# Gates added into HBM cells by the transfers, the norm's factor moved ahead of the expert product, expert searches and row products started earlier

## The reference

```python
q = (xf @ w_q).reshape(n, PEER_HEADS, 2, PEER_DK // 2)
s = jnp.einsum('nhpd,hpkd->nhpk', q, sub_keys).astype(jnp.float32)
sv, si = lax.top_k(s, PEER_TOPK)
cand = (sv[:, :, 0, :, None] + sv[:, :, 1, None, :]).reshape(n, PEER_HEADS, PEER_TOPK * PEER_TOPK)
...
tv, tsel = lax.top_k(cand, PEER_TOPK)
eidx = jnp.take_along_axis(cidx, tsel, axis=-1).reshape(n, PEER_HEADS * PEER_TOPK)
g = jax.nn.softmax(tv, axis=-1).reshape(n, PEER_HEADS * PEER_TOPK).astype(xn.dtype)
...
act = jax.nn.gelu(jnp.einsum('nd,ned->ne', xt, u[it]), approximate=False) * gt
return jnp.einsum('ne,ned->nd', act, v[it])
```

## Time and profile before

| what | value |
|---|---|
| time, median of 3 runs | 2144.63 us (2143.15 to 2148.9) |
| the profiled execution, first to last instruction | 2142.5 us |
| PE busy | 2066.5 us, 96% |
| DVE busy | 1525.4 us, 71% |
| ACT busy | 858.8 us, 40% |
| POOL busy | 596.8 us, 28% |
| DMA, mean over the span | 232 GB/s |

### The profile page before, as it was taken

How to read it: one execution, slowest core, us unless ns; L and a number is a source line. 1 busy time by engine, 2 the same in 40 slices (tenths; PEclk the granted TensorE clock), 3 DMA queues, 4 the chain that set the end, 5 groups by cost and what they waited for, 6 DMA issues and landing times.

```text
span 2142.5 us, 29919 instructions
## 1 busy us (share of the span) xinstructions
PE 2066.5 (96%) x11202; PEld 1790.2 (84%) x11202; DVE 1525.4 (71%) x2689; ACT 858.8 (40%) x898; POOL 596.8 (28%) x426
## 2 busy tenths in 40 slices
PE   7999997998799999999999999999999999999997
PEld 6987774997799888888888888878787888888886
DVE  5988744454533989888899986666776777677765
ACT  4330135333333454444554444434333443344343
POOL 2000000220400005676576768001222212212300
PEclk9999996999899999999999999999999999999999
DMA  5453481442244566656666566788888888988974
GB/s 201 174 183 136 170 336 59 144 170 99 98 138 156 191 215 212 217 202 220 211 211 216 204 208 250 259 317 324 310 345 340 327 334 324 354 349 327 365 251 143
DMA packets 89310, 497.69 MB, mean 232 GB/s; under 512 B 16672, under 2 KB 16816, under 8 KB 35920
## 3 DMA queue, kind: packets, MB, share of 16 engines
q1 hardware_dynamic: 65904, 406.83, 52.4%
q0 software_dynamic: 18672, 72.87, 9.3%
q10 hardware_dynamic: 4656, 17.04, 2.0%
HBM read 457.78 MB, written 38.13 MB: 231 GB/s over the span
## 4 chain that ended last, share of the span: by engine, by line
PE 88%; DMA 4%; DVE 4%; ACT 2%; issue 1%; POOL 0%; SPq 0%; DVEq 0%; ACTq 0%; POOLq 0%
PE acc L1291 21%; PE mis L1531 14%; PE acc L1531 14%; PE acc L1292 11%; PE acc L1272 6%; PE acc L1274 5%; PE acc L1273 5%; PE acc L1317 4%; DMA raw<-in_v 4%; PE acc L1414 3%; DVE wl L739 1%; PE mis L1386 1%; ACT wh L457 1%; PE mis L1362 1%; DMA gin<-G 1%
## 5 line engine op out<-in xcount | busy, mean ns | idle before, releaser
L739 DVE TENSOR_TENSOR wl<-raw,wh 128x2048 fp32r<-128x2048 f32 x310 | 708.7, 2288 | 315.0 <-ACT wh L457 310.2
L457 ACT ACTIVATE wh<-raw 128x2048 fp32r<-128x2048 f32 x310 | 592.8, 1913 | 426.1 <-DMA raw<-in_v 397.9
L1291 PE MATMUL acc<-xhl,wh 128*128 128x512 f32 x2048 | 715.4, 393 | 2.6 <-DVE wl L739 2.6
L1292 PE MATMUL acc<-xhl,wl 128*128 128x256 f32 x2048 | 576.1, 281 | 0.0
L1638 POOL DMA_INDIRECT G<-gsum,cell x256 | 371.6, 1452 | 393.1 <-DVE same L1107 318.2
L1291 PEld LDWEIGHTS acc<-xhl,wh 128*128 128x128 f32 x2048 | 384.8, 188 | 89.1 <-DVE wl L739 2.9
L1292 PEld LDWEIGHTS acc<-xhl,wl 128*128 128x128 f32 x2048 | 387.2, 189 | 0.0
L1272 PE MATMUL acc<-xhl,wh 128*128 128x288 f32 x768 | 231.8, 302 | 23.9 <-DVE wl L775 13.9
L1273 PE MATMUL acc<-xhl,wh 128*128 128x288 f32 x768 | 229.0, 298 | 0.0
L1274 PE MATMUL acc<-xhl,wl 128*128 128x288 f32 x768 | 228.0, 297 | 0.0
L644 ACT ACTIVATE hsum<-acc 128x256 f32<-128x256 f32 x128 | 49.2, 385 | 344.2 <-PE acc L1292 328.3
(11 more groups left out here) (261 smaller groups left out, 2537.6 us busy)
## 6 DMA issues: line engine op xcount, KB each, us to landing
raw<-in_u SPq DMA_DIRECT2D x128, 1024.0 KB
raw<-in_v SPq DMA_DIRECT2D x128, 1024.0 KB
raw<-in_w_mix SPq DMA_DIRECT2D x28, 1024.0 KB
G<-zero SPq DMA_DIRECT2D x16, 1024.0 KB, 13.9
raw<-in_w_out SPq DMA_DIRECT2D x16, 1024.0 KB
raw<-in_w_pq SPq DMA_DIRECT2D x16, 1024.0 KB
h<-hbg ACTq DMA_DIRECT2D x32, 512.0 KB
hin<-h SPq DMA_DIRECT2D x32, 512.0 KB
```

What stands on the lines that cost most here:

```text
L457: act.activation(wh[:, n % 4], raw[:, n % 4], ACT.Copy).then_inc(hi_done, 1)
L739: dve.tensor_tensor(wl[:, n % 4], raw[:, n % 4], wh[:, n % 4].bitcast(F32), ALU.subtract).then_inc(lo_done, 1)
L1291: pe.matmul(acc[:, s, :].rearrange("p (a n) -> p a n", a=2), wh[:, s, j, :], xhl[:, :, j, 0:NU], start=(j == 0), stop=False)
L1292: ins = pe.matmul(acc[:, s, 0:NU], wl[:, s, j, :], xh[:, j, 0:NU], start=False, stop=(j == DT - 1))
```

## The change

1. **Gates.** `gate_sum` and its tiles are gone. The scatters carry `compute_op=ALU.add` and take each head's own gates from `gij`: the transfer adds to the cell. Number (256), size and waits on earlier scatters stay.
2. **The norm's factor.** At the start of PQ, POOL computes `xn` = h * rstd for the prompt tokens (4 instructions of 128x1024). In PQ's last slot ACT and DVE write `xh` and `xl` anew from it (16 each of 128x256), each group of four when PE has used it for the last time in PQ (`xn_free`). U slot 0 waits for `xl` one block at a time. DVE's second operation per U slot goes: it adds bank and `hsum` straight into `hbg`. The scores of PQ's last slot are taken behind U slot 0.
3. **Searches.** Heads come first: head 0 is searched under PQ slots 4 to 12, unit 2 (head 1) in slots 11 and 12, part 0 of unit 3 in slot 14; the sample units follow in U slots 2 to 6; the heads 2 to 7 then take 9 slots each from slot 8 on, against 12.
4. **Row products.** `DOTS_U` goes from 6 to 24: the products lie in every second slot from U slot 81 to V slot 14. The v rows are added from V slot 17 on, 8 in 25 slots. `XROW_IT` goes from 26 to 18.

```diff
-XROW_IT, HST_IT = 26, 27
+XROW_IT, HST_IT = 18, 27
-SAMPLE_SLOTS, HEAD_SLOTS = 6, 12
+SAMPLE_UNIT, SAMPLE_PAIR = 16, 8
+FIRST_PARTS = {4: (0, 0), 6: (0, 1), 7: (1, 0), 9: (1, 1), 11: (2, 0), 12: (2, 1), 14: (3, 0)}
+SAMPLE_PARTS = {2: (16, 0), 3: (16, 1), 5: (17, 0), 6: (17, 1)}
+HEAD0_SLOT, HEAD_SLOTS = 8, 9
-DOTS_U = 6
+DOTS_U = 24
-V_ADDS = {V_GELU + 1 + 15 * n // 8: n for n in range(PICKS)}
+V_ADDS = {V_GELU + 1 + 25 * n // 8: n for n in range(PICKS)}
...
+            def normal_hi():
+
+                for j in range(DT):
+                    if j % 4 == 0:
+                        act.wait_ge(xn_ready, j // 4 + 1)
+                        if j < 12:
+                            act.wait_ge(xn_free, j // 4 + 1)
+                        else:
+                            act.wait_ge(slot_used, U0)
+                    split(xh[:, j, 0:NU], xn[:, j, :], par[:, Q_GFFN + j:Q_GFFN + j + 1])
...
+                    if i == 3 and s == 3:
+                        normal_lo()
                     slot_ready(PQ0, i, s)
                     if not (first and s < 2):
                         dve.wait_ge(pq_score, 4 * i + s - 1)
                     dve.tensor_tensor(qp[:, s % 2, :], acc[:, s, 0:N], rstd[:, 1, :], ALU.mult).then_inc(acc_free, 1)
-
-            for i in range(4):
-                pq(i, i == 0)
+                    first_heads(4 * i + s)
+
+            def normal_lo():
+
+                for j in range(DT):
+                    split(xl[:, j, 0:NU], xn[:, j, :], par[:, Q_GFFN + j:Q_GFFN + j + 1], xh[:, j, 0:NU], 3 * DT + CT + j + 1)
...
-                dve.tensor_tensor(hadd[:, s % 2, :], acc[:, s, 0:NU], hsum[:, s % 2, :], ALU.add).then_inc(acc_free, 1)
-                dve.wait_ge(acc_free, slot_no(U0, it, s) + 5)
-                dve.tensor_tensor(hbg[:, s, :], hadd[:, s % 2, :], rstd[:, 1, 0:NU], ALU.mult).then_inc(scaled, 1)
+                dve.wait_ge(half_out, 4 * it + s + 1)
+                dve.tensor_tensor(hbg[:, s, :], acc[:, s, 0:NU], hsum[:, s % 2, :], ALU.add).then_inc(acc_free, 1)
...
-            def gate_sum(h, m):
-
-                t, r, n = m // K16, m % K16, 2 * K16 * h + m
-                if m == 0:
-                    own.wait(0)
-                if n >= 2:
-                    dve.wait_ge(sums_ready, n - 1)
-                gates = gij[:, 0, 2:UNITS, :].rearrange("p (h t) r -> p h t r", t=2)[:, 0:h + 1, t, :]
-                dve.scalar_tensor_tensor(same[:, n % 2, 0:h + 1, :], expert[:, 0:h + 1, t, :], expert[:, h, t, r:r + 1], gates,
-                                         ALU.is_equal, ALU.mult, accum_out=gsum[:, h, t, r:r + 1]).then_inc(sums_ready, 1)
...
                 for j in range(DT):
+                    if first:
+                        pe.wait_ge(split_lo, 3 * DT + CT + j + 1)
...
-            with pe.Fori(0, XROW_IT) as i:
+            for s in range(4):
+                u_slot(0, s, s == 0)
+                if s == 0:
+                    scores(3, 3, False)
+            with pe.Fori(1, XROW_IT) as i:
...
-            pool.wait_ge(const_in, 16)
+            pool.wait_ge(rstd_done, 4)
+            for a in range(4):
+                pool.tensor_tensor(xn[:, 4 * a:4 * a + 4, :], hT[:, 4 * a:4 * a + 4, 0:NU], bcast(rstd[:, 1, 0:NU], 4, 1), ALU.mult).then_inc(xn_ready, 1)
...
                     for r in range(K16):
-                        if r % 4 == 0:
-                            pool.wait_ge(sums_ready, 2 * K16 * h + K16 * t + r + 4)
-                        pool.indirect_dma_start(cells_of, bass.IndirectOffsetOnAxis(ap=cell[:, h, t, r:r + 1], axis=0), gsum[:, h, t, r:r + 1],
-                                                None).then_inc(scattered[t], 16)
+                        pool.indirect_dma_start(cells_of, bass.IndirectOffsetOnAxis(ap=cell[:, h, t, r:r + 1], axis=0), gij[:, 0, 2 * h + t, r:r + 1],
+                                                None, compute_op=ALU.add).then_inc(scattered[t], 16)
```

More of the change, by code:

```diff
@@ L634, in u_iteration @@
                         gelu_of(it - 1)
-                    if hook:
+                    if hook and not (isinstance(it, int) and it == 0):
                         hook(s)
                     half_evac(4 * it + s)
+                    if hook and isinstance(it, int) and it == 0:
+                        hook(s)
             def half_evac(n):
@@ L1141, in route_head @@
                         dve.sem_inc(routed, 1)
[L1142 to L1147 removed]
+                if k == 0 and 2 < h <= HEADS:
+                    gates_and_cells(h - 1)
+            for i in range(4):
+                pq(i, i == 0)
             for n in range(124):
                 lo_next(U0, n // 4, n % 4)
[L1150 to L1161 removed]
+                second_head(n)
+                route_sample(n)
+                if n >= HEAD0_SLOT:
+                    route_head(2 + (n - HEAD0_SLOT) // HEAD_SLOTS, (n - HEAD0_SLOT) % HEAD_SLOTS)
                 if n == 4 * XROW_IT - 4:
@@ L1264, in _, with product @@
         def _(pe):
-            def product(out, w, mh, ml, n, before=None):
+            def product(out, w, mh, ml, n, before=None, freed=None):
                 wr, blocks = w
@@ L1274, in product, with slot @@
                     ins = pe.matmul(out, wl[:, wr, b, :], mh(j), start=False, stop=(j == n - 1))
+                    if freed and j % 4 == 3 and j < n - 1:
+                        ins.then_inc(freed, 1)
                 return ins
-            def slot(base, i, s, mh, ml, cols=N, before=None, stride=4):
+            def slot(base, i, s, mh, ml, cols=N, before=None, stride=4, freed=None):
                 g = slot_no(base, i, s, stride)
@@ L1282, in slot, with u_slot @@
                 product(acc[:, s % 4, 0:cols], (s % 4, lambda j: j), lambda j: mh[:, j, 0:cols], lambda j: ml[:, j, 0:cols],
-                        DT, before).then_inc(slot_used, 1)
-            def u_slot(i, s):
+                        DT, before, freed).then_inc(slot_used, 1)
+            def u_slot(i, s, first=False):
                 g = slot_no(U0, i, s)
@@ L1462, in pq @@
                 for s in range(4):
-                    slot(PQ0, i, s, xh, xl)
+                    slot(PQ0, i, s, xh, xl, freed=xn_free if i == 3 and s == 3 else None)
                     if first and s == 0:
@@ L1469, in pq @@
                         scores(i, s - 1, first)
-                scores(i, 3, first)
+                if i < 3:
+                    scores(i, 3, first)
             def scores(i, s, first):
@@ L1494, in _ @@
             ins.then_inc(xrow_turned, 1)
-            for i in range(XROW_IT, HST_IT):
+            with pe.Fori(XROW_IT, HST_IT) as i:
                 for s in range(4):
```

134 lines of the change are left out of this document (74 added, 60 removed).

## The result

The changed kernel takes 2246.03 us (median of 4 runs, 2240.39 to 2249.52) against 2146.77 us (4 runs, 2143.15 to 2151.81) for the kernel before: 1.0453 times as long, interval [1.0428, 1.0478]. The forecast of 2139.4 us was wrong, and so was its range, whose upper end was 2194. The profiled execution has a span of 2247.7 us, 105.2 more than before.

A forecast was written before the change was run, and what follows sets the result against it. U and V were taken as bound by PE's own matmuls. From 2142.5 us of span, gains of 1.1 and 4.1 gave 2137.3; with the median 2.1 above the span, 2139.4 us, range 2134 to 2194.

The forecast's parts named there:

- What bounds the kernel: U and V: bound by PE's own matmuls; freeing DVE returns at most 9.0 us of PE waits plus the clock.
- Gate sums removed: U slots: 73 us less DVE work where PE never waited for DVE; worth nothing by itself.
- The second operation per U slot: End of U: three removed DVE operations of 0.38 us end the first V slot's wait earlier; gain 1.1 us.
- The row products: 18 moved from V to U: shortens V's waits for wl; gain 4.1 us, bounds 1 to 4.6.
- xn, operands and early searches: PQ's end and U's start: hidden, PE not held; cost 0, up to 3 us if the searches' reserve is missed.
- Rival B: Early searches hold PE at U slot 0 or around slot 9, cancelling the gain: 2142 to 2146 us; chance 0.16.
- rival C: End of U: the clock is kept as well; 2132 us in full, 2135.5 with half beyond the sum; chance 0.12.
- the forecast's own case: Scatter additions hidden, gains of 1.1 and 4.1 us: span 2137.3, median 2139.4 us; chance 0.40.
- The scatters: POOL's queue: adding costs 0.05 us more per scatter, 13 us in all, hidden; upper end 0.37 each, costing 73 us.
- rival A: Adding scatter dearer than 0.09 us: gather 2 late, PE stands at U slot 88; 2168 to 2212 us; chance 0.32.
- the reserve of 22 us: Gather 2 lands at 1156, needed by 1178 before PE is held at U slot 88: 0.09 us per scatter.
- the forecast's formula: Loss from late gather 2: 256 times the extra cost per scatter, less 22 us; 73 us at 0.37.

The follow-up runs named there:

- the plain variant: The changed kernel with plain scatters in place of adding ones, so gates of an expert chosen by several heads aren't summed: 2137.63 us, ratio 0.9958 to before.
- after: The profiled execution of the changed kernel with the whole change, adding scatters included: span 2247.7 us, median 2246.03 us, ratio 1.0453 to before.

## Why the prediction was wrong

**What bounds the kernel: right.** PE's busy time stayed, and what was lost is waits of PE and the clock behind them; of what the plain variant won, 1.5 us aren't located.

**Gate sums removed, worth 0: nothing speaks against it.** PE was busy for all of U's 460 us from 700 to 1160 before as well, so there was nothing to win there; no run takes the sums out and leaves all else, so what the run with plain scatters and 6 products won beyond the clock can't be given to them or denied.

**The second operation per U slot, 1.1 us: nearly right.** In the plain variant DVE's chain from the product with G to the last emptying takes 1421.54 - 1405.05 = 16.5 us, where it took 17.8. G came 0.45 us later, so the first V matmul starts 0.9 us earlier (1422.01 against 1422.89). PE's two waits there fell by less, from 4.4 to 4.0 us (2.8 and 1.2, where the forecast had about 2.2 and 1.1).

**The row products, 4.1 us: right.** V's waits for `wl` went from 4.6 us to 0.4 in after and to 1.1 in the plain variant, and the pair with 24 and with 6 products in U differs by 4.5 to 5.2 us.

**xn, operands and early searches, 0: right.** PE starts U slot 0 at 693.5 us, where 693.1 was worked out, and is busy without a gap from there to 1166.5, slot 9 included. Rival B is gone. xn's products, to which the forecast gave no size, take 3.4 us each on POOL (2.4 to 4.5), in a place where nothing waits for them.

**The clock (rival C): half of it came.** From 1390 to 1430 us the plain variant has 0.96 against 0.91, 40 x 0.05 = 2 us. Before, the clock was low a second time behind PE's idle time of 1.8 us at the first V slot, 0.75 and 0.77; behind 1.25 us in the plain variant it is 1.00. The same two stretches, before and then in the plain variant (columns as in the earlier trace rows):

```profile
1422.90:1426.00 3.10, 3.10 (x11) 2.55 (x12) 0.40 (x1) 1.06 (x1) 0.81 (x1) 0.75 1.02 410
1426.00:1430.00 4.00, 4.00 (x30) 4.00 (x29) 0.00 (x0) 0.21 (x1) 0.00 (x0) 0.77 0.99 393
```

```profile
1422.90:1426.00 3.10, 3.10 (x24) 2.85 (x23) 0.00 (x0) 0.20 (x1) 0.00 (x0) 1.00 1.01 386
1426.00:1430.00 4.00, 4.00 (x39) 4.00 (x38) 0.00 (x0) 0.00 (x0) 0.00 (x0) 1.00 1.02 417
```

With plain scatters the forecast's own case is met: 2134.6 us of span against 2137.3 forecast, 2137.63 against 2139.4 as a median. Of the 7.9 us of span that were won, 0.9 are the earlier start of V, 3.5 are V's waits and about 2 the clock; the other 1.5 aren't located. Against its own kernel before (2147.65) the plain variant won more than the 5.2 us forecast, 9 us by the ratio, with an interval from 5.8 to 12.2. (The forecast's case C with half of the rest comes to 2139.4 - 3.7 = 2135.7, not 2135.5.)

**The scatters: the step that failed.** The forecast's rate for plain scatters was right (1.80 us worked out, (1132.4 - 681.4) / 255 = 1.77 measured), and so was the mechanism of rival A: a late gather, and behind its row product the emptying and the `wl` that PE wants. The failed term is the cost of the addition on POOL. "I take 0.05, as nothing but one more read is asked per cell", with an upper end of 0.37. Measured: 0.58 us alone, 0.68 beside a `wl`, and 2.51 - 1.77 = 0.74 us in the rate with DVE at work. Two errors stand behind it and a third beside it.

The first is what was taken as a bound. The 0.37 us was the difference between an indirect and a direct issue of 128 pieces, read as a price of working out addresses. Nothing in the trace said that the adding form would be a sum of the parts already seen; no row of an adding form existed. A difference between two known forms doesn't bound a third one. The row that could have served as an upper end, though no more than a guess either, was the whole of the plain issue, 0.96 us: the addition might have cost another one. By that 256 x 0.96 - 22 = 224 us would have been the far end, and the measured 105 lies well inside.

The second is that only gather 2 was timed against its product. The forecast's reserve was that of the last 256 scatters; gather 0 stands behind 224 of them and is wanted four slots earlier. PE was held for it at 1166.5, so it had (1166.5 - 5 - 7.4 - 681) / 224 = 2.11 us per scatter, 0.31 above the forecast's plain rate. At the measured 2.51 it is missed as well, and then most of the loss is there (64.9 of 107.8 us), since DVE stops at the first product that isn't there.

The third is the reserve of 22 us, which was too small. It didn't matter, since the cost above it was missed by more. PE is held four slots behind a missing product (85 behind 81, 89 behind 85), not three. And gather 2 couldn't have been issued at 1148, since it waits for row product 0. In the plain variant the last scatter ends at 1133.4 and POOL then stands until that product is done:

```profile
1156.62 0.97 POOL L1670 DMA_INDIRECT ring<-in_ur,eidx  x1 [23.21 <-DVE hs L1136]
```

So POOL could have been later by about 694 + 89 x 5.56 - 5 - 7.4 - 1133.7 = 43 us, or 0.17 us per scatter, before gather 2 held PE. That is an estimate; the addition's 0.74 lies far beyond either figure. With it the forecast's formula gives 256 x 0.74 - 22 = 167 us, and 146 with 43 for the reserve. 107.8 were lost because POOL speeds up as soon as DVE stands still (1.85 us from scatter to scatter).

The chances had the mechanism at 0.32, against 0.40 for no effect. That a term which decides the sign rests on no row at all was said, but the value was then chosen as if its lower end were the nearest row.

The Trainium skill ("SBUF — State Buffer", section "Who interferes with whom") infers that a tensor_tensor doesn't stall descriptor generation. The rows of after go against it once more: 1.54 us alone and 3.42 beside `wl` at 992.40. The kernel that was meant to free DVE kept it in `wl` for as long as before (715.0 us against 708.7), and an issue beside a `wl` was lengthened as before, by 1.9 us where it had been 1.8.

## What to carry to other kernels

Before work is moved from an engine with slack into a DMA's form, find out what one issue of that form costs the engine that issues it, and if no trace shows one, allow for a surcharge as large as the whole of the nearest issue, not a difference of two (here that would have covered what was measured). On an in-order queue that carries both bulk issues and a few urgent ones, time every urgent one against its consumer, the first above all, and against what it waits for itself. Placing the bulk between the urgent ones, with fewer early row products and 32 of the 256 additions spared, brought this kernel from 2246.03 to 2139.77 us. And a rate read from a stretch in which the other engine stood still is not the rate that holds when the stall is cured (1.85 against 2.51 us).

## What the runs showed of the hardware

- An indirect DMA with an addition occupies GpSimd for 1.54 to 1.55 us at 128 cells and 1.43 at 64; the plain one for 0.96 and 0.89. The addition's 0.5 to 0.6 us hardly depend on the number of cells.
- It puts more packets on the queue, 144 per scatter of 128 cells and 80 per scatter of 64, against 32 for a plain one of 128 (3680 for 114 scatters from 800 to 1000 us in the plain variant), at the same bytes.
- No landing of an adding scatter was waited for in after: all of POOL's idle time between scatters is the 0.30 us of an issue (77.7 us in 255 times), though each head waits for the landings of the one before.
- Beside a 128x2048 `wl` on VectorE a plain scatter's issue takes 2.74 us for 0.96 and an adding one's 3.42 for 1.54.
- When PE comes back from an idle time of 65 us, the granted clock is 0.50 (1.2 GHz) for the next 4.7 us, 0.91 over the 5 us behind them and then 1.00; after 43 us it goes the same way (0.50, 0.88, 1.00). This cost 3 us each time, beside the idle times themselves. Behind 1.8 us of idle time at the first V slot of the kernel before it is 0.75 and 0.77, and behind 1.25 us in the plain variant 1.00.
